# Two expert units per layer fetched in three transfers, split by rows

## The reference

```python
def hier_moe(h, wg, bg, we, be, w_gate, w_up, w_down):
    ...
    for e in range(N_EXPERTS):
        hid = jax.nn.silu(t @ w_gate[e]) * (t @ w_up[e])
        y = y + combine[:, e:e + 1] * (hid @ w_down[e]).astype(jnp.float32)
...
for l in range(DEPTH):
    ...
    h = h + mixed @ w_out[l]
    h = h + cross_attention(rms_norm(h, norm_cross[l]), rms_norm(mem, norm_mem[l]), ...)
    h = h + hier_moe(rms_norm(h, norm_ffn[l]), ...)
```

## Time and profile before

| | us |
|---|---|
| median of three runs | 873.65 |
| lowest, highest | 873.0, 873.66 |
| span of the profiled execution | 871.5 |
| TensorE busy in it | 825.5 |
| VectorE, ScalarE busy | 370.7, 174.8 |
| what the median has beyond the span | 2.15 |

### The profile page before, as it was taken

One profiled execution on the slowest core, in us unless ns is written; L12 is line 12 of the kernel. 1 busy time (PEld: TensorE's weight loads), 2 busy tenths in 40 slices (PEclk: granted clock), 3 DMA queues, 4 the chain that ended last, 5 costly groups with the idle time before them and its releaser, 6 DMA issues.

```text
span 871.5 us, 12659 instructions
## 1 busy us (share of the span) xinstructions
PE 825.5 (95%) x5396; PEld 561.8 (64%) x5396; DVE 370.7 (43%) x652; ACT 174.8 (20%) x406; POOL 13.6 (2%) x21
## 2 busy tenths in 40 slices
PE   9999999999999999988989999999999999787785
PEld 8998986679664666535637898766976544332533
DVE  4669876464752111100105896734565411110102
ACT  2212125411240000000012113451133100000003
POOL 0140000000000000000000000000000000000000
PEclk9999999999999999999999999999999999988899
DMA  9953175276489999999999316608858999999995
GB/s 353 421 225 121 55 290 194 69 315 253 180 340 396 429 427 424 428 427 426 427 419 424 136 50 247 237 1 321 357 214 334 363 426 425 429 428 427 428 421 226
DMA packets 26057, 272.65 MB, mean 313 GB/s; under 512 B 3216, under 2 KB 3600, under 8 KB 7440
## 3 DMA queue, kind: packets, MB, share of 16 engines
q1 hardware_dynamic: 24560, 270.26, 75.4%
q10 hardware_dynamic: 1440, 1.56, 0.6%
HBM read 270.76 MB, written 1.05 MB: 312 GB/s over the span
## 4 chain that ended last, share of the span: by engine, by line
PE 77%; DMA 20%; SPq 1%; DVE 1%; issue 1%; ACT 0%; DVEq 0%; PEld 0%; PEldq 0%; ACTq 0%
DMA early<-in_expert_units 20%; PE bank L720 10%; PE bank L855 8%; PE bank L801 6%; PE bank L1084 6%; PE bank L1260 6%; PE bank L1333 6%; PE bank L829 4%; PE bank L895 4%; PE bank L907 3%; PE bank L1011 3%; PE bank L787 2%; PE bank L779 2%; PE bank L1292 2%; PE bank L1273 2%; PE bank L1069 2%
## 5 line engine op out<-in xcount | busy, mean ns | idle before, releaser
L855 PE MATMUL bank<-ring,xT 128*32 128x512 f32 x560 | 67.5, 621 | 8.7 <-DMA ring<-in_expert_units 8.5
L855 PE MATMUL bank<-early,xT 128*32 128x512 f32 x464 | 57.3, 633 | 13.2 <-DMA early<-in_expert_units 13.2
L2576 DVE TENSOR_TENSOR hid<-hid,bank 128x256 f32<-128x256 f32 x16 | 6.7, 421 | 139.1 <-ACT hid L1816 139.1
L829 PE MATMUL bank<-sel,hn 128*128 128x128 f32 x448 | 56.7, 289 | 6.0 <-issue 6.0
L829 PEld LDWEIGHTS bank<-sel,hn 128*128 128x128 f32 x448 | 55.4, 205 | 7.2 <-issue 7.2
L801 PE MATMUL bank<-ring,uT 128*128 128x512 f32 x128 | 55.9, 592 | 0.0
L907 PE MATMUL bank<-yy,states 128*128 128x512 f32 x112 | 54.6, 617 | 0.0
L2581 DVE COPY yy<-bank 128x512 f32<-128x512 f32 x14 | 9.7, 692 | 97.2 <-PE bank L895 97.2
L855 PEld LDWEIGHTS bank<-ring,xT 128*32 128x32 f32 x560 | 17.6, 112 | 51.0 <-issue 40.5
L720 PE MATMUL bank<-uT,ring 128*128 128x256 f32 x224 | 49.4, 380 | 0.0
L855 PEld LDWEIGHTS bank<-early,xT 128*32 128x32 f32 x464 | 14.5, 113 | 51.4 <-issue 37.9
(11 more groups left out here) (388 smaller groups left out, 1322.4 us busy)
## 6 DMA issues: line engine op xcount, KB each, us to landing
ring<-in_expert_units SPq DMA_DIRECT2D x45, 2048.0 KB, 23.3
early<-in_expert_units SPq DMA_DIRECT2D x37, 2048.0 KB, 25.5
ring<-in_fixed_units SPq DMA_DIRECT2D x20, 2048.0 KB, 12.8
ring<-in_fixed_units SPq DMA_DIRECT2D x16, 1024.0 KB, 19.7
ring<-in_expert_units SPq DMA_DIRECT2D x12, 1024.0 KB, 6.5
early<-in_expert_units SPq DMA_DIRECT2D x11, 1024.0 KB, 39.6
early<-in_expert_units SPq DMA_DIRECT2D x10, 512.0 KB, 6.9
ring<-in_fixed_units SPq DMA_DIRECT2D x4, 512.0 KB, 4.8
```

The costliest lines, as they stand in the source:

```text
L829: mm = pe.matmul(bank[half][:, c * P:c * P + P], hn[:, t, half * 4 + c], sel[:, t].rearrange("p e s -> p (e s)"), start=(t == 0), stop=(t ...
L855: mm = pe.matmul(bank[2][32 * e:32 * e + 32, :], xT[:, 2 * n + c, 32 * e:32 * e + 32], w[:, e, :, c], start=(n == 0 and c == 0), stop=(n = ...
```

## The change

Two units of each layer are fetched by three transfers in place of one. `PARTED_ROWS` names them: in each layer the first unit in the ring that belongs to quad 3 or a later one, and the first that belongs to quad 5 or a later one. These are units 21 and 30 in the first layer and units 24 and 36 in the second. The first transfer has rows 0 to 111, the second rows 112 to 119, the third rows 120 to 127. All three count up the semaphore of the same buffer, and `more_loads` adds to what TensorE waits for, 16 for each additional transfer that this buffer has had.

```diff
+PARTED_ROWS = [next(n for n, unit in enumerate(RING_ORDER) if unit[0] == lay and isinstance(unit[1], int) and unit[1] >= quad * UNITS_PER_QUAD)
+               for lay in range(L) for quad in (3, 5)]
+ROWS = (slice(0, 112), slice(112, 120), slice(120, P))
+
+
+def more_loads(n):
+
+    return (len(ROWS) - 1) * sum(m % RING == n % RING and m <= n for m in PARTED_ROWS)
...
@@ static_unit
+                if n in PARTED_ROWS:
+                    dst, src = expert_unit(lay, name, ring[slot])
+                    for rows in ROWS:
+                        sp.dma_start(dst[rows], src[rows]).then_inc(unit_in[slot], 16)
+                    return
                 if isinstance(name, int):
                     dst, src = expert_unit(lay, name, ring[slot])
...
@@ wait_number
-                pe.wait_ge(unit_in[n % RING], base + LOADED * (n // RING + 1))
+                pe.wait_ge(unit_in[n % RING], base + LOADED * (n // RING + 1 + more_loads(n)))
```

## The result

The changed kernel takes 906.89 us (median of five runs, 905.62 to 910.45), the kernel before, on the same chip, 873.66 us (five runs, 873.0 to 874.71). The ratio is 1.0389, with a 95% interval of 1.0376 to 1.0402. The forecast was 874.25 us, in a range of 871.5 to 876.2 us. The profiled execution took 909.3 us and spans 907.5 us, 36.0 us more than the one before. It lies 2.4 us above the median, so its own differences add up to 36 us and not to 33.

The account below looks back on a forecast made before the run. The prediction took TensorE to bound the kernel outside the expert stretches and the weight stream at their ends. Issues and TensorE added 0, uneven rows +0.3 us per layer: 873.65 + 0.6 = 874.25 us, range 871.5 to 876.2 us.

Parts of the forecast that it names:

- The step that failed: In the four units' transfers, each engine takes 0.612 us a row, from 4.895 us for eight rows in a whole unit.
- The 112 rows: First transfer of each of the four units: seven rows on each of 16 engines, at 0.612 us a row.
- Who carries the eight rows: Two eight-row transfers of each unit: the same eight engines carry both, chosen between bounds of 0 and 9.2 us a unit.
- halves A and B: DMA engines in parted units: eight (A) get nine rows, 0.612 us later; eight (B) get seven, 0.612 us earlier.
- 0.93 us of lead: At each layer's last landing, one half's latest engine leads the other's by one instruction packet: +0.3 us per layer.
- +-1.22 us a layer: Two parted units per layer before the late waits: one half of the engines 1.22 us later, the other 1.22 us earlier.
- The upper one: Eight-row transfers, most: each part on one engine, which has 7 + 16 rows; 9.2 us late per unit, some 37 us in all.
- few engines: Rival on the eight-row transfers: each part on one or two engines, 17 to 37 us slower; chance 0.02.
- landings several microseconds late: Sign in the profile after that the forecast is wrong: a landing this late would mean parts on few engines.
- burden on the late: Rival: both layers' latest engine is among those with nine rows; +1.22 us at each layer's last landing, 876.1 us; chance 0.22.
- The issues are hidden: SP's eight more DMAs, 0.328 us each: the queue's backlog hides up to 0.8 us per unit, so 0.
- the delay D: How far A's latest engine leads B's; under 2.45 us, the last landing moves by +1.22 - D; if more, by -1.22 us.

Follow-up runs that it names:

- e7: Changed kernel, but the four units fetched in two transfers, rows 0 to 63 and 64 to 127: 903.55 us, 1.0352 of the kernel before.
- e12: Changed kernel, but of the four units only rows 112 to 119 and 120 to 127 fetched, in two transfers: 874.71 us, 1.0002 of the kernel before.
- e3: Changed kernel, but only rows 0 to 111 of the four units fetched, in one transfer: 892.18 us, 1.0210 of the kernel before.
- e1: Changed kernel, but the four units' three transfers cut by columns, all 128 rows in each: 874.99 us against 873.74 us before.
- e16: Changed kernel, but the four units' three transfers take even rows, rows 1, 5, 9..., and rows 3, 7, 11...: 873.75 us, 1.0000 of the kernel before.
- e11: Changed kernel, but the four units fetched in two transfers, even rows and odd rows: 873.96 us, 1.0007 of the kernel before.
- e17: Changed kernel, but only rows 0 to 119 of the four units fetched, in one transfer: 902.12 us, 1.0321 of the kernel before.
- e14: Changed kernel, but the four units' even SBUF rows come from HBM rows 0 to 63, odd ones from 64 to 127: 873.80 us, 1.0001 of before.
- e15: Changed kernel, but the four units' SBUF rows 0 to 63 come from even HBM rows, 64 to 127 from odd ones: 903.93 us, 1.0362 of before.
- e8: Changed kernel, but only unit 21 cut, into sixteen transfers: SBUF rows four apart from eight neighbouring HBM rows: 882.27 us, 1.0097 of before.
- e6: Changed kernel, but only unit 21 cut, into sixteen transfers of eight rows four apart, in SBUF and HBM: 885.05 us, 1.0136 of before.

## Why the prediction was wrong

**The step that failed** is in the part on the change: "The whole unit of 128 rows is eight rows on each of 16 engines: 4.895 / 8 = 0.612 us a row. 112 rows are seven on each." The 0.612 us is right for whole units, and was carried over to rows that other engines bring to other places. That became the base of the whole sum: after it, only the count of rows on an engine could differ, and the answer had to be a few times 0.612 us. The mean row in the two stretches took 0.87 and 1.20 us, and in the experiments a row takes twice (e7) or four times (e12) 0.61 us. The sum gave 0.6 us; the term that it lacked is 8.3 us a unit.

**The 112 rows** were priced at less than in a whole unit, seven rows instead of eight on every engine. Alone they cost 4.6 us a unit (e3), over half of the whole.

**Who carries the eight rows** was chosen between two bounds: eight engines, "the same ones for both parts". The number is right, since each part adds eight packets. That they are the same engines can't be seen. It was the point on which the text spent most of its care, halves A and B, the latest engine of each, 0.93 us of lead; its terms of +-1.22 us a layer drown in 15 to 21 us.

**The bounds.** The upper one, 9.2 us a unit and 37 us in all, would have held the result (33 us), but for another reason: a part on one engine. It got a chance of 0.02 as "few engines", and the range left it out. The landings several microseconds late that were named as its sign came, and so did eight packets for each part, which exclude it if each stands for an engine. The text also says that no row of the trace shows a transfer of eight rows, and yet bounds only the number of rows on an engine, with 0.612 us for each: by the trace, the time of a row in such a transfer had no upper bound.

**Engines 7 and 15**, named for the rival "burden on the late": the row of the Trainium skill in "DMA: Bandwidth & Descriptors", section "Latency and other measured facts", calls their slowness specific to transfers whose descriptors software writes. The queue here is q1 hardware_dynamic, and no run shows an engine by number, so this added nothing to the rival.

**The rival that was left out.** The rule on ports that the Trainium skill has in "SBUF — State Buffer", section "Door 1: The DMA port swizzle", speaks against the change as a rival: rows 112 to 127 lie in four of the sixteen sets, and by it, as an estimate, eight engines writing eight rows in two sets pass at a quarter of the pace. Worked out with the row time of before: eight rows, four to a path, take 4 x 0.612 = 2.45 us, both parts 4.9 us, and e12 shows them at 4.9 + 0.3 = 5.2 us, to within about 0.4 us. With the 112 rows ahead at 7 x 0.612 = 4.3 us, a rival of +4.3 us a unit and 17 us in all would have stood in the text, half of the measured 33 us.

**What was right.** The kernel is bound at the ends of the expert stretches by the stream: each microsecond lost there came back undiminished, 20.87 us at all waits behind unit 30, 20.87 + 15.40 = 36.27 us at the end, against 36.0 us of span. The issues are hidden (305.94 against 305.86 us). The number of transfers costs next to nothing (e1: 1.25 us for eight more; e16: 0.3 us). That a free three-way cut (e16) comes close to the forecast of +0.6 us is no merit of the sum: its 0.6 us came from nine rows on half of the engines, and e16 has rows that can be dealt out eight to each. No run tests that term or the delay D by itself.

## What to carry to other kernels

A full DMA stream is measured by its rate under a share of 1.00, and not by gaps: in the slow stretches here the engines were busy throughout and moved 209 to 315 GB/s in place of 427. When a transfer of 128 long rows into the SBUF is cut in a full stream like this one, cut by columns, or by rows such that each part has equally many in each of the sixteen sets (every second or every fourth row), not by neighbouring rows: the one cost 0.1 to 0.3 us for each 2-MiB unit, the other 7 to 8 us. Before a duration is carried over to an operation of another shape, ask what of it belongs to the shape, and bound it anew.

## What was not expected of the hardware

- A transfer of 64 rows at even places of 128 runs at 425 to 432 GB/s, one of 64 neighbouring rows at 264 to 293 GB/s, with the same packets (e11, e7). A row takes 0.61 us in the one and 1.13 to 1.29 us in the other, once it has settled.
- Two transfers of eight rows of 16 KB (1/8 of a unit) take as long as the whole 128 rows: 874.71 against 873.66 us (e12). And a whole transfer right behind them is slowed too, from 0.31 us a row to as much as 1.53 us.
- 120 rows in one transfer cost 7.1 us a unit, more than the 4.6 us of 112 rows (e17, e3). Fifteen engines with eight rows each are worse than sixteen with seven, if the packets are read rightly.
- Which rows of HBM are read made no difference of note: 873.8 against 873.96 us, 903.93 against 903.55 us (e14, e11; e15, e7). Only between the combs, e8 and e6, stand 2.8 us that nothing here explains.
